# A seven-product up projection for the feed-forward part of a two-layer hybrid encoder

## The chip, the cores and the metric

The kernel runs on one core of a Trainium2 chip. The time is device microseconds of one execution. Its engines are named as in the profile: PE (TensorE), DVE (VectorE), ACT (ScalarE), POOL (GpSimd), and SP, the queue that issues most DMAs. Every engine works through its own instructions in order and waits for others at semaphores.

## What is computed

The encoder has two layers over 16 meta tokens and 1024 input tokens of width 1024, all in fp32. In each layer an input projection feeds four mixers (a short convolution, sliding-window attention, retention, RWKV), an output projection and a layer norm follow, and then the feed-forward part with another norm. The change is in the feed-forward part:

```python
def conv_glu_ffn(h, w_up, conv_w, w_down):
    z = causal_dwconv(h @ w_up, conv_w)
    u, gate = jnp.split(z, 2, axis=-1)
    return (jax.nn.silu(gate) * u) @ w_down
```

`h` is tokens x 1024, `w_up` 1024 x 5632, `w_down` 2816 x 1024, and the convolution has three taps along the tokens.

## The kernel before, in words

The tokens of a layer are four chunks: one of 272 (16 meta and 256 others) and three of 256. Layer and chunk make eight **units**, u = 0 to 7; units 0 and 4 are the first chunks. Activations lie transposed in SBUF (`hT`: 8 feature blocks of 128 partitions by tokens). Weights are read again for each unit: SP loads tiles of 128 x 1024 fp32 (0.524 MB, 4 KB a partition, one output block of 128 features by 8 input blocks) into a ring of five slots, in the order of the table `USES`. A tile is loaded once the block that used the slot before is done.

The order of blocks on PE is written out in `all_blocks`: for each unit the output projection (`out0` to `out7`), the input projection of the next unit (25 blocks), then the **up phase** (`up0` to `up43`) and the **down phase** (`dn0` to `dn7`). Each block goes to PSUM bank 0 or 1 in turn; PE waits until the block two before has been taken out (`bank_free`), which ACT does for the projections and DVE for `out` and `dn`. Semaphore `blk` counts blocks, `evA` and `evV` what ACT and DVE have taken out.

In the up phase, a block is 8 matmuls of 128x128 weights by all tokens of the unit. ACT saves the last two columns for the next chunk's convolution and copies the block into one of four rows of `raw`. DVE applies the three taps in three instructions and multiplies with the gate, ACT computes the silu. Side programs run beside it: the RWKV, retention and attention work of the next unit is cut into steps by `yield`, and `together` issues one step of each after each step of the main program, on every engine in the same order.

POOL does little: for each unit it builds three masked operands of the RWKV part (`rwkv` on POOL), after a wait for DVE (`w_mask1`) and with `w_pool` as its result, and near the end it stores the output by DMA. PE's side step waits for `w_pool`. At the start PE runs 22 warm-up matmuls of a 128x128 constant (`WARM`, L1507).

```python
for f in range(NUP):
    rest(dense(u, f"up{f}", h))
    yield
```

## Time and profile before

| | |
|---|---|
| median of 3 runs | 3187.67 us (3187.49 to 3188.24) |
| profiled execution, span | 3186.1 us |
| PE, DVE, ACT busy | 3159.8, 1340.6, 878.3 us |
| POOL busy | 34.1 us |
| moved by DMA | 442.15 MB, mean 139 GB/s |

The runs are timed without a profile and the span is that of one profiled execution; of that execution no other time is given. "Busy" counts overlapping instructions of an engine once. A matmul's duration holds its way through the array, so two that follow each other overlap: what one costs is read from starts, or from a piece of the chain by its count.

### The profile page before, as it was taken

The page shows a single profiled execution, that of the slowest core. Times are in us where ns is not written, and L with a number is a line of the kernel's source. Part 1 is how long each engine was busy: PE and PEld are TensorE (multiplying, and loading weights), DVE is VectorE, ACT ScalarE, POOL GpSimd, SP SyncE. Part 2 cuts the span into 40 slices and gives each one's busy share as a digit, 9 for nine tenths or more (in the row PEclk, how much of TensorE's full clock was granted, in tenths as well). Part 3 has the DMA queues.
Part 4 walks back from the last instruction along what each step waited for, and adds up shares of the span by engine and source line. Part 5 has one row for each costly group of instructions (what it writes and reads, how often), then busy time and mean ns, then how long its engine had stood idle before and what let it go on. Part 6 is the DMA issues. An engine that isn't in the chain of part 4 may idle for free.

```text
span 3186.1 us, 51716 instructions
## 1 busy us (share of the span) xinstructions
PE 3159.8 (99%) x21708; PEld 2695.2 (85%) x21708; DVE 1340.6 (42%) x3192; ACT 878.3 (28%) x2644; POOL 34.1 (1%) x47
## 2 busy tenths in 40 slices
PE   9999999999999999999999999999999999999998
PEld 7788788888888888888888888888888888888887
DVE  4345551545515354163541635415453254532541
ACT  3323430324303242042430423204241043411320
POOL 0000000000000000000000000000000000000000
PEclk9999999999999999999999999999999999999999
DMA  6244344443444434444344443444334443344443
GB/s 218 85 139 131 100 133 142 148 149 103 139 152 148 142 107 151 152 147 132 107 126 153 152 131 107 152 152 152 125 127 152 156 148 119 127 153 164 163 153 114
DMA packets 137574, 442.15 MB, mean 139 GB/s; under 512 B 14832, under 2 KB 34416, under 8 KB 137088
## 3 DMA queue, kind: packets, MB, share of 16 engines
q1 hardware_dynamic: 136192, 434.65, 42.4%
q0 software_dynamic: 1152, 4.19, 0.4%
q8 instruction: 173, 2.83, 0.4%
q14 instruction: 57, 0.47, 0.1%
HBM read 427.14 MB, written 4.19 MB: 135 GB/s over the span
## 4 chain that ended last, share of the span: by engine, by line
PE 97%; DVE 2%; ACT 1%; issue 0%; DMA 0%; SPq 0%; POOL 0%; DVEq 0%; ACTq 0%
PE psum L957 67%; PE psum L1471 19%; PE psum L951 2%; PE psum L973 1%; PE psum L1233 1%; PE psum L1245 1%; PE psum L1258 1%; PE psum L1184 1%; PE psum L1306 1%; PE psum L1415 1%; PE psum L1398 0%; ACT prpt L844 0%; PE psum L1353 0%; PE psum L1367 0%; PE psum L1371 0%; PE psum L1133 0%
## 5 line engine op out<-in xcount | busy, mean ns | idle before, releaser
L957 PE MATMUL psum<-hT,slots 128*128 128x256 f32 (+2 forms) x8832 | 1986.6, 383 | 2.1 <-ACT hT L593 2.1
L957 PEld LDWEIGHTS psum<-hT,slots 128*128 128x128 f32 x8832 | 1660.8, 190 | 261.3 <-issue 16.1
L1471 PE MATMUL psum<-gT,slots 128*128 128x256 f32 (+1 forms) x2816 | 615.3, 381 | 0.0
L1471 PEld LDWEIGHTS psum<-gT,slots 128*128 128x128 f32 x2816 | 534.0, 190 | 77.5
L1576 DVE SCALAR_TENSOR_TENSOR hT<-hT,psum 128x256 f32<-128x256 f32 (+2 forms) x128 | 54.1, 423 | 612.8 <-PE psum L1471 504.1
L885 ACT ACTIVATE last<-psum 128x2 f32<-128x2 f32 x352 | 60.1, 171 | 857.7 <-PE psum L957 856.9
L957 PE MATMUL psum<-mixT,slots 128*128 128x256 f32 (+2 forms) x1024 | 226.2, 381 | 0.0
L957 PEld LDWEIGHTS psum<-mixT,slots 128*128 128x128 f32 x1024 | 194.6, 190 | 28.4
L2046 DVE TENSOR_SCALAR tmpG<-raw,par 128x256 f32<-128x256 f32 (+2 forms) x176 | 62.4, 355 | 364.5 <-ACT raw L886 364.4
L604 ACT ACTIVATE scr<-hT 128x256 f32<-128x256 f32 (+2 forms) x120 | 47.8, 421 | 586.5 <-DVE hT L1594 565.5
L2046 DVE TENSOR_SCALAR gT<-raw,par 128x256 f32<-128x256 f32 (+2 forms) x176 | 62.3, 354 | 306.9 <-ACT raw L886 306.8
L886 ACT ACTIVATE raw<-psum 128x256 f32<-128x256 f32 (+2 forms) x352 | 133.9, 380 | 0.0
L2050 DVE SCALAR_TENSOR_TENSOR tmpG<-raw,par,tmpG 128x256 f32<-128x256 f32 (+2 forms) x176 | 86.5, 491 | 6.3
L2048 DVE SCALAR_TENSOR_TENSOR tmpG<-raw,par,tmpG 128x256 f32<-128x256 f32 (+2 forms) x176 | 86.4, 491 | 6.3
L2050 DVE SCALAR_TENSOR_TENSOR gT<-raw,par,gT 128x256 f32<-128x256 f32 (+2 forms) x176 | 85.8, 487 | 6.3
L2048 DVE SCALAR_TENSOR_TENSOR gT<-raw,par,gT 128x256 f32<-128x256 f32 (+2 forms) x176 | 85.7, 487 | 6.3
L580 ACT ACTIVATE rows<-psum 128x256 f32<-128x256 f32 (+1 forms) x80 | 31.0, 387 | 181.2 <-PE psum L957 181.2
L1636 DVE TENSOR_TENSOR gT<-rows 128x256 f32<-128x256 f32 (+1 forms) x56 | 24.1, 430 | 130.6 <-ACT rows L636 77.0
L878 ACT ACTIVATE tmpG<-tmpG 128x256 f32<-128x256 f32 (+2 forms) x176 | 73.8, 419 | 12.8 <-DVE tmpG L2050 12.4
L2040 DVE TENSOR_TENSOR gT<-gT,tmpG 128x256 f32<-128x256 f32 (+2 forms) x176 | 74.0, 421 | 1.2
L618 ACT ACTIVATE hT<-hT,par 128x256 f32<-128x256 f32 (+2 forms) x120 | 60.7, 589 | 39.0 <-DVE hT L1614 39.0
L580 ACT ACTIVATE gT<-psum 128x256 f32<-128x256 f32 (+1 forms) x56 | 21.5, 384 | 128.9 <-PE psum L957 128.9
(260 smaller groups left out, 2255.7 us busy)
## 6 DMA issues: line engine op xcount, KB each, us to landing
slots<-in_weights SPq DMA_DIRECT2D x792, 512.0 KB, 3.4
hT<-in_x SPq DMA_DIRECT2D x8, 512.0 KB, 5.1
out<-prpt POOLq DMA_DIRECT2D x8, 512.0 KB, 3.1
tab<-in_tables SPq DMA_DIRECT2D x6, 512.0 KB, 5.3
raw<-rows SPq DMA_DIRECT2D x24, 128.0 KB, 2.4
gT<-rows SPq DMA_DIRECT2D x24, 64.0 KB, 2.0
con<-in_consts SPq DMA_DIRECT2D x1, 1434.0 KB, 10.8
tab<-in_tables SPq DMA_DIRECT2D x2, 544.0 KB, 5.5
```

The source lines that it names most:

```text
L618: act(hT[:, m, t0:t0 + n], hT[:, m, t0:t0 + n], ACT.Identity, bias=gb[:, KD + m:KD + m + 1], scale=gb[:, m:m + 1]).then_inc(S["ln_hT"], 1)
L878: act(tmpG[:, m % 2, :n], tmpG[:, m % 2, :n], ACT.Silu).then_inc(S["g_silu"], 1)
L885: act(last2[:, u % 2, f, :], psum[:, i % 2, n - 2:n], ACT.Copy)
L886: act(buf[:, 2:2 + n], psum[:, i % 2, :n], ACT.Copy).then_inc(S["evA"], 1)
L951: return pe.transpose(dst, src, ident[:n, :n])
L957: ins = mm(psum[:, i % 2, :n], lhsT, rhs, start=k == 0, stop=k == len(pairs) - 1)
L1471: ins = mm(psum[:, i % 2, :n], w[:, e * P:(e + 1) * P], gT[:, k, first:first + n], start=k == 0, stop=k == KF - 1)
L1576: stt(x, x, ALPHA, psum[:, i % 2, :n], ALU.mult, ALU.add).then_inc(S["evV"], 1)
L2040: tt(gT[:, m, :n], gT[:, m, :n], tmpG[:, m % 2, :n], ALU.mult).then_inc(S["glu"], 1)
L2046: k = step(ts(y, src[:, 2:2 + n], par[:, w + 2:w + 3], None, ALU.mult))
L2048: k = step(stt(y, src[:, 1:1 + n], par[:, w + 1:w + 2], y, ALU.mult, ALU.add))
L2050: stt(y, src[:, 0:n], par[:, w:w + 1], y, ALU.mult, ALU.add).then_inc(S["fconv"], 1)
```

## The change

Units 1, 2, 3, 5, 6 and 7 (`seven(u)`) compute the up projection in a form of fast matrix multiplication; units 0 and 4 keep the old one. The 44 output blocks are 11 groups of 4. In a group the weights are a 2 x 2 matrix of blocks A11, A12, A21, A22 (two output blocks by four input blocks each), the activations a 2 x 2 matrix (four feature blocks by 128 tokens). Seven products of such blocks replace eight, and each is 8 matmuls of 128 columns into half a bank. The order is `STEPS7`.

Four of the products use sums of weight blocks (S1 to S4). POOL makes these in HBM (`wsum`, 11 x 4 x 0.524 MB a layer): `copy_blocks` issues 12 DMAs from HBM to HBM, `sum_blocks` 12 accumulating ones in three rounds, and POOL waits for the copies, round one and round two before what follows. Those of layer 0 stand between POOL's masks of unit 0 and unit 1, those of layer 1 between the masks of unit 1 and unit 2. SP waits for a layer's sums before its first load of one, in units 1 and 5. Four sums of activations (`tsum`) are made by DVE, late in the next unit's input projection, for unit 7 in unit 6's down phase.

Some products fall into the same PSUM range and accumulate there (`start` only for s = 0, 1, 5). ACT copies products 0, 1, 2 and 6 into `raw` (1 and 6 negated); DVE adds or subtracts products 3, 4 and 5 onto rows of `raw` straight out of PSUM, and copies the halo columns. `raw` has eight rows, and DVE convolves a group while the next is multiplied. The up phase of a changed unit has 77 weight tiles instead of 44. The DMA descriptor scratch is set smaller, which makes room in SBUF.

```diff
+def seven(u):
+
+    return u % NCH != 0
+
+
+GROUPS = NUP // 4
+FAST = [u for u in range(NU) if seven(u)]
+STEPS7 = ["A11", "S1", "S2", "S4", "S3", "A12", "A22"]
+SUMS = ["S1", "S3", "S2", "S4"]
+SUM_PARTS = [(0, 4), (4, 8), (8, GROUPS)]
+
+
+def up_names(u):
+
+    return [f"us{g}_{s}" for g in range(GROUPS) for s in range(7)] if seven(u) else [f"up{f}" for f in range(NUP)]
+
...
-    return name[:3] == "out" or name[:2] == "dn"
+    return name[:3] == "out" or name[:2] == "dn" or name[:2] == "us" and name[-1] in "345"
...
-        raw = sb("raw", 4 * (CW + 2))[:, :].rearrange("p (r t) -> p r t", r=4)
+        raw = sb("raw", 8 * (CW + 2))[:, :].rearrange("p (r t) -> p r t", r=8)
+        tsum = sb("tsum", 2048)[:, :].rearrange("p (j k t) -> p j k t", j=4, k=4)
+        wsum = nc.dram_tensor("wsum", (DEPTH, GROUPS, 4, P, 1024), F32, kind="Internal").ap()
...
+        def product_at(base, s):
+
+            return bank((base + s) % 2)[:, 0:2 * P]
...
-                sp.dma_start(slots[:, i % SLOTS, :], weights[l, which]).then_inc(s_slot[i % SLOTS], 16)
+                if name[:2] == "us":
+                    if name == "us0_1" and u == l * NCH + 1:
+                        done = 16 * len(SUM_PARTS) * (l + 1)
+                        sp.wait_ge(S["ws_first"], 2 * done)
+                        sp.wait_ge(S["ws_second"], done)
+                        sp.wait_ge(S["ws_third"], done)
+                    source = weights[l, which] if STEPS7[int(name[-1])][0] == "A" else wsum[l, which[0], which[1]]
+                else:
+                    source = weights[l, which]
+                sp.dma_start(slots[:, i % SLOTS, :], source).then_inc(s_slot[i % SLOTS], 16)
...
+            def copy_blocks(l):
+
+                for part in SUM_PARTS:
+                    for kind, first in (("S1", "A21"), ("S3", "A11"), ("S2", "A11"), ("S4", "A12")):
+                        g.dma_start(block_of(l, kind, part), block_of(l, first, part)).then_inc(S["ws_copy"], 16)
+
+            def sum_blocks(l):
+                n = len(SUM_PARTS)
+                g.wait_ge(S["ws_copy"], 16 * 4 * n * (l + 1))
+                for part in SUM_PARTS:
+                    for kind, more in (("S1", "A22"), ("S3", "A21")):
+                        g.dma_start(block_of(l, kind, part), block_of(l, more, part), accum_op=ALU.add).then_inc(S["ws_first"], 16)
+                g.wait_ge(S["ws_first"], 16 * 2 * n * (l + 1))
+                for part in SUM_PARTS:
+                    g.dma_start(block_of(l, "S2", part), block_of(l, "S1", part), accum_op=ALU.add).then_inc(S["ws_second"], 16)
+                g.wait_ge(S["ws_second"], 16 * n * (l + 1))
+                for part in SUM_PARTS:
+                    g.dma_start(block_of(l, "S4", part), block_of(l, "S2", part), accum_op=ALU.add).then_inc(S["ws_third"], 16)
+
             rwkv(0)
+            copy_blocks(0)
+            sum_blocks(0)
             for u in range(NU):
                 if u + 1 < NU:
                     rwkv(u + 1)
+                if u == 0:
+                    copy_blocks(1)
+                    sum_blocks(1)
...
+                if seven(u):
+                    for g in range(GROUPS):
+                        base, r0 = AT[u, f"us{g}_0"], 4 * (g % 2)
+                        one, two = raw[:, r0:r0 + 2, :], raw[:, r0 + 2:r0 + 4, :]
+                        a.wait_ge(S["fconv"], NUP * u + max(4 * g - 4, 0))
+                        act(raw[:, r0:r0 + 4, 0:2], last2[:, (u - 1) % 2, 4 * g:4 * g + 4, :], ACT.Copy)
+                        dst = {0: one[:, :, 2:2 + P], 1: two[:, :, 2 + P:2 + 2 * P], 2: one[:, :, 2 + P:2 + 2 * P], 6: two[:, :, 2:2 + P]}
+                        for s in range(7):
+                            src = product_at(base, s).rearrange("p (m t) -> p m t", m=2)
+                            if s in (0, 1, 2, 6):
+                                a.wait_ge(S["blk"], base + s + 1)
+                            if s in (1, 6):
+                                act(dst[s], src, ACT.Identity, scale=-1.0).then_inc(S["evA"], 1)
+                            elif s in (0, 2):
+                                act(dst[s], src, ACT.Copy).then_inc(S["evA"], 1)
+                            if g and s in (2, 4):
+                                silu(2 * g - 2 + (s == 4))
+                            if s in (1, 3, 5, 6):
+                                yield
...
+            def up_by_seven(u, h):
+
+                old, new = [x[:, 0:P] for x in h], [x[:, P:2 * P] for x in h]
+                t1, t3, t2, t4 = ([tsum[:, j, k, :] for k in range(4)] for j in range(4))
+                moving = [old[:4], t1, t2, new[4:], t3, old[4:], t4]
+                for g in range(GROUPS):
+                    base = AT[u, f"us{g}_0"]
+                    for s in range(7):
+                        w = next_slot()
+                        bank_free(base + s)
+                        if g == 0 and s == 1:
+                            pe.wait_ge(S["tsum"], 4 * (FAST.index(u) + 1))
+                        dst = product_at(base, s)
+                        for e in range(2):
+                            for k in range(4):
+                                ins = mm(dst[:, e * P:(e + 1) * P], w[:, (4 * e + k) * P:(4 * e + k + 1) * P], moving[s][k],
+                                         start=s in (0, 1, 5) and e == 0 and k == 0, stop=k == 3, skip_group_check=True)
+                        ins.then_inc(S["blk"], 1)
...
+                tt(tsum[:, 0], b11, b12, ALU.subtract).then_inc(S["tsum"], 1)
+                yield
+                tt(tsum[:, 1], b22, b12, ALU.subtract).then_inc(S["tsum"], 1)
+                yield
+                v.wait_ge(S["tsum"], before + 2)
+                stt(tsum[:, 2], tsum[:, 1], -1.0, b11, ALU.mult, ALU.subtract).then_inc(S["tsum"], 1)
+                yield
+                v.wait_ge(S["tsum"], before + 3)
+                stt(tsum[:, 3], tsum[:, 2], -1.0, b21, ALU.mult, ALU.subtract).then_inc(S["tsum"], 1)
...
+                            if g and s < 3:
+                                for f in ((4 * g - 4, 4 * g - 3), (4 * g - 2,), (4 * g - 1,))[s]:
+                                    conv(f, raw[:, 4 * ((g - 1) % 2) + f % 4, :])
+                            if s == 3:
+                                v.wait_ge(S["evA"], FREED[base + 2])
+                                v.wait_ge(S["blk"], base + 4)
+                                tt(one[:, :, 2 + P:2 + 2 * P], one[:, :, 2 + P:2 + 2 * P], part[3], ALU.add).then_inc(S["evV"], 1)
+                            if s == 4:
+                                v.wait_ge(S["blk"], base + 5)
+                                tt(two[:, :, 2 + P:2 + 2 * P], two[:, :, 2 + P:2 + 2 * P], part[4],
+                                   ALU.subtract).then_inc(S["evV"], 1)
+                                v.wait_ge(S["evV"], FREED[base + 4])
+                                v.tensor_copy(last2[:, u % 2, 4 * g:4 * g + 4, :], raw[:, r0:r0 + 4, 2 * P:2 * P + 2])
+                            if s == 5:
+                                v.wait_ge(S["blk"], base + 6)
+                                tt(one[:, :, 2:2 + P], one[:, :, 2:2 + P], part[5], ALU.add).then_inc(S["evV"], 1)
+                            if g and s in (3, 5):
+                                glu(2 * g - 2 + (s == 5))
+                            if s == 6:
+                                v.wait_ge(S["evA"], FREED[base + 6])
+                                v.wait_ge(S["evV"], FREED[base + 5])
+                            if s in (1, 3, 5, 6):
+                                yield
...
+    up = up.reshape(DEPTH, GROUPS, 2, 2, P, 2, 4, P).transpose(0, 1, 2, 5, 4, 3, 6, 7)
...
-    nc = bacc.Bacc("TRN2", target_bir_lowering=False, num_devices=1)
+    nc = bacc.Bacc("TRN2", target_bir_lowering=False, num_devices=1, dynamic_dma_scratch_size=2048)
```

The places where the order moves are these. PE, at the start of unit 1's up phase, before (L957 is the matmul of all projections, L1165 and L951 are side work):

```order
L957 MATMUL psum<-hT,slots 128x256 [waits evA,slot1_loaded]
L957 MATMUL psum<-hT,slots 128x256 x7
L957 MATMUL psum<-hT,slots 128x256 [waits evA,slot2_loaded,ln_hT]
L957 MATMUL psum<-hT,slots 128x256 x7
L1165 MATMUL psum<-con,rows 128x64 [waits w_yc,w_znew,w_yTc,n_var_out,smallA,n_mean_out,smallV]
L1165 MATMUL psum<-con,rows 128x64 x31
L951 MATMUL psum<-con,rows 128x128 [waits r_qd,evA,r_rope,smallA,in_hT,a_mix]
L951 MATMUL psum<-con,rows 128x128 x3
L957 MATMUL psum<-hT,slots 128x256 [waits evA,slot3_loaded]
L957 MATMUL psum<-hT,slots 128x256 x7
```

and now (L1577 is the new product, L1262 and L1048 the same side work):

```order
L1577 MATMUL psum<-hT,slots 128x128 [waits evA,slot2_loaded,ln_hT]
L1577 MATMUL psum<-hT,slots 128x128 x7
L1577 MATMUL psum<-tsum,slots 128x128 [waits tsum,evA,slot3_loaded]
L1577 MATMUL psum<-tsum,slots 128x128 x7
L1262 MATMUL psum<-con,rows 128x64 [waits w_yc,w_znew,w_yTc,n_var_out,smallA,n_mean_out,smallV]
L1262 MATMUL psum<-con,rows 128x64 x31
L1048 MATMUL psum<-con,rows 128x128 [waits r_qd,evA,r_rope,smallA,in_hT,a_mix]
L1048 MATMUL psum<-con,rows 128x128 x3
L1577 MATMUL psum<-tsum,slots 128x128 [waits evA,slot4_loaded]
L1577 MATMUL psum<-tsum,slots 128x128 x7
L1577 MATMUL psum<-hT,slots 128x128 [waits evA,slot0_loaded]
L1577 MATMUL psum<-hT,slots 128x128 x7
```

Each side step stands behind two products of half the columns, and the second product needs `tsum`. On POOL, from the masks of unit 0 on (`w_mask1` is DVE's mask), before:

```order
L544 TENSOR_TENSOR wset<-wset,con 128x8x64 [waits w_mask1]
L546 TENSOR_TENSOR wset<-wset,con 128x512 [waits w_unit]
L549 TENSOR_TENSOR wset<-wset,con 128x512 [waits w_t0]
L544 TENSOR_TENSOR wset<-wset,con 128x8x64 [waits w_mask1]
L546 TENSOR_TENSOR wset<-wset,con 128x512 [waits w_unit]
L549 TENSOR_TENSOR wset<-wset,con 128x512 [waits w_t0]
```

and now:

```order
L591 TENSOR_TENSOR wset<-wset,con 128x512 [waits w_t0]
L615 DMA wsum<-in_weights 128x4x1024 x8
L615 DMA wsum<-in_weights 128x3x1024 x4
L622 DMA wsum<-in_weights 128x4x1024 [waits ws_copy]
L622 DMA wsum<-in_weights 128x4x1024 x3
L622 DMA wsum<-in_weights 128x3x1024 x2
L625 DMA wsum<-wsum 128x4x1024 [waits ws_first]
L625 DMA wsum<-wsum 128x4x1024
L625 DMA wsum<-wsum 128x3x1024
L628 DMA wsum<-wsum 128x4x1024 [waits ws_second]
L628 DMA wsum<-wsum 128x4x1024
L628 DMA wsum<-wsum 128x3x1024
L586 TENSOR_TENSOR wset<-wset,con 128x8x64 [waits w_mask1]
```

The 24 DMAs of layer 0 now stand between the masks of unit 0 and unit 1, with a wait ahead of each round.

## Rows read from the trace of the kernel before

**Rows 1.** The page: span, busy shares, granted clock.
```profile
span 3186.1 us, 51716 instructions
PE 3159.8 (99%) x21708; PEld 2695.2 (85%) x21708; DVE 1340.6 (42%) x3192; ACT 878.3 (28%) x2644; POOL 34.1 (1%) x47
...
PEclk9999999999999999999999999999999999999999
```

**Rows 2.** The page: the chain that ended last, by engine and line.
```profile
PE 97%; DVE 2%; ACT 1%; issue 0%; DMA 0%; SPq 0%; POOL 0%; DVEq 0%; ACTq 0%
PE psum L957 67%; PE psum L1471 19%; PE psum L951 2%; PE psum L973 1%; PE psum L1233 1%; PE psum L1245 1%; PE psum L1258 1%; PE psum L1184 1%; PE psum L1306 1%; PE psum L1415 1%; PE psum L1398 0%; ACT prpt L844 0%; PE psum L1353 0%; PE psum L1367 0%; PE psum L1371 0%; PE psum L1133 0%
```

**Rows 3.** The chain in time, 820 to 970 us: start us, us, what.
```profile
824.12 58.71 PE psum L957 x272
```

**Rows 4.** Groups by line and form, PE and PEld: busy us, mean ns.
```profile
L957 PE MATMUL psum<-hT,slots 128*128 128x256 f32 x6624 | 1470.2, 381 | 0.0
...
L957 PE MATMUL psum<-hT,slots 128*128 128x258 f32 x704 | 158.7, 383 | 0.0
...
L957 PEld LDWEIGHTS psum<-hT,slots 128*128 128x128 f32 x8832 | 1660.8, 190 | 261.3 <-issue 16.1 <-ACT hT L593 2.4
```

**Rows 5.** Warm-up: chain in time, all its records, durations, then DMA there.
```profile
10.49 2.12 PE psum L1507 x19
...
5.76 7.29 PE psum L1507 x44
...
L1507 PEld LDWEIGHTS psum<-con x20: 192/192/192, 10.3 to 12.4; 128*128 128x128 f32 x20
...
10.20:12.60 2.40, 2.40 (x23) 2.40 (x23) 1.00 1.02 415
```

**Rows 6.** The chain in time, 690 to 720 us, two pieces of up products.
```profile
700.86 3.65 PE psum L957 x16
...
710.95 3.46 PE psum L957 x16
```

**Rows 7.** Groups by form: DVE over the span, then ACT from 695 to 878 us.
```profile
L2050 DVE SCALAR_TENSOR_TENSOR gT<-raw,par,gT 128x256 f32<-128x256 f32 x132 | 64.0, 485 | 4.7
...
L2046 DVE TENSOR_SCALAR gT<-raw,par 128x256 f32<-128x256 f32 x132 | 46.5, 353 | 227.5 <-ACT raw L886 227.4
...
L1576 DVE SCALAR_TENSOR_TENSOR hT<-hT,psum 128x256 f32<-128x256 f32 x104 | 43.7, 421 | 509.3 <-PE psum L1471 432.2 <-PE psum L957 77.0
...
L1865 DVE TENSOR_TENSOR wset<-psum,con 128x512 f32<-128x512 f32 x24 | 16.4, 683 | 8.7 <-PE psum L1194 6.8 <-PE psum L1184 1.9
...
L883 ACT ACTIVATE raw<-last 128x2 f32<-128x2 f32 x42 | 8.6, 204 | 0.0
...
L885 ACT ACTIVATE last<-psum 128x2 f32<-128x2 f32 x41 | 7.0, 171 | 87.3 <-PE psum L957 87.2
```

**Rows 8.** Busy us of the engines in three stretches, clock, DMA share, GB/s.
```profile
core 0: us, PE busy (x) PEld busy (x) DVE busy (x) ACT busy (x) POOL busy (x), PEclk, DMA share, GB/s
117.00:310.00 193.00, 191.39 (x1758) 158.40 (x1757) 96.36 (x230) 61.90 (x164) 3.23 (x3) 1.00 0.39 123
310.00:710.00 400.00, 398.80 (x2646) 332.50 (x2648) 167.18 (x391) 115.24 (x335) 3.24 (x3) 1.00 0.41 134
695.00:878.00 183.00, 181.19 (x1675) 153.44 (x1674) 94.73 (x221) 72.03 (x237) 3.24 (x3) 1.00 0.37 120
```

**Rows 9.** Timeline of POOL: start us, us, what, idle before and its end.
```profile
115.70 1.10 POOL L549 TENSOR_TENSOR wset<-wset,con 128x512 f32<-128x512 f32 x1
299.98 1.09 POOL L544 TENSOR_TENSOR wset<-wset,con 128x512 f32<-128x512 f32 x1 [183.17 <-DVE wset L1865]
```

**Rows 10.** Timeline of PE: the first side matmuls that read POOL's result.
```profile
313.05 1.15 PE L1233 MATMUL psum<-wset 64*64 64x64 f32 x32
```

**Rows 11.** DMA issues: KB each, median us from issue to landing.
```profile
slots<-in_weights SPq DMA_DIRECT2D x792, 512.0 KB, 3.4
...
out<-prpt POOLq DMA_DIRECT2D x8, 512.0 KB, 3.1
```

More of the change, by code:

```diff
@@ L138, in all_blocks @@
         out += [(u + 1, name) for name in in_order(u + 1)]
-        out += [(u, f"up{f}") for f in range(NUP)]
+        out += [(u, name) for name in up_names(u)]
         if u == NU - 2:
@@ L142, in all_blocks @@
         out += [(u, f"dn{m}") for m in range(KD)]
-    out += [(NU - 1, f"up{f}") for f in range(NUP)]
+    out += [(NU - 1, name) for name in up_names(NU - 1)]
     return out + [(NU - 1, f"dn{m}") for m in range(KD)]
@@ L190, in all_uses @@
         elif name[:2] == "up":
-            out.append((l, N_IN + KD + int(name[2:]), u, name, None))
+            f = int(name[2:])
+            if f % 2 == 0:
+                out += [(l, N_IN + KD + f + half, u, f"up{f + 1}", None) for half in range(2)]
+        elif name[:2] == "us":
+            g, s = map(int, name[2:].split("_"))
+            kind = STEPS7[s]
+            if kind[0] == "A":
+                out.append((l, N_IN + KD + 4 * g + {"A11": 0, "A12": 1, "A22": 3}[kind], u, name, None))
+            else:
+                out.append((l, (g, SUMS.index(kind)), u, name, None))
         elif name == "dn0":
@@ L519, in _ @@
                     load_input(i - 3, sp)
-                if name == "up0" and u == NU - 1:
+                if name == "us0_0" and u == NU - 1:
                     sp.wait_ge(S["blk"], AT[NU - 1, "out7"] + 1)
@@ L878, in silu @@
                     act(tmpG[:, m % 2, :n], tmpG[:, m % 2, :n], ACT.Silu).then_inc(S["g_silu"], 1)
+                if seven(u):
[17 more added lines that the diff above has]
+                                yield
+                    silu(KF - 2)
+                    silu(KF - 1)
+                    return
                 for f in range(NUP):
@@ L1454, in up @@
                 pe.wait_ge(S["ln_hT"], KD * (nth_norm(2 * u) + 1))
-                for f in range(NUP):
-                    rest(dense(u, f"up{f}", h))
-                    yield
+                if seven(u):
+                    yield from up_by_seven(u, h)
+                    return
+                for f in range(0, NUP, 2):
+                    w = [next_slot(), next_slot()]
+                    for e in range(2):
+                        rest(feature(u, f"up{f + e}", [(w[k // 4][:, 512 * e + k % 4 * P:512 * e + (k % 4 + 1) * P], h[k])
+                                                       for k in range(KD)]))
+                        yield
[11 more added lines that the diff above has]
+                        dst = product_at(base, s)
+                        for e in range(2):
+                            for k in range(4):
[4 more added lines that the diff above has]
+                            yield
             def down(u):
@@ L1618, in project @@
                 l, c0 = layer_of(u), u % NCH == 0
+                sums = token_sums(u - 1) if u and seven(u - 1) else iter(())
                 mu_at = {name: i for i, name in enumerate(["r0", "r1", "k0", "k1", "v0", "v1", "lo"])}
@@ L1741, in project @@
                         rest(short_conv(u, int(name[2])))
+                    if i >= 18:
+                        next(sums, None)
                     if name == "sq0":
@@ L2050, in up @@
                     stt(y, src[:, 0:n], par[:, w:w + 1], y, ALU.mult, ALU.add).then_inc(S["fconv"], 1)
+                if seven(u):
+                    for g in range(GROUPS):
+                        base, r0 = AT[u, f"us{g}_0"], 4 * (g % 2)
+                        one, two = raw[:, r0:r0 + 2, :], raw[:, r0 + 2:r0 + 4, :]
+                        part = [product_at(base, s).rearrange("p (m t) -> p m t", m=2) for s in range(7)]
+                        for s in range(7):
+                            if g and s < 3:
[19 more added lines that the diff above has]
+                                v.wait_ge(S["evV"], FREED[base + 5])
+                            if s in (1, 3, 5, 6):
+                                yield
+                    for f in range(NUP - 4, NUP):
+                        conv(f, raw[:, 4 * ((GROUPS - 1) % 2) + f % 4, :])
+                        if f % 2:
+                            glu(f // 2)
+                    return
@@ L2051, in up @@
+                for f in range(NUP):
+                    m, s = divmod(f, 2)
+                    v.wait_ge(S["evA"], FREED[AT[u, f"up{f}"]])
+                    conv(f, raw[:, f % 4, :])
                     if s and m:
@@ L2065, in down @@
                         ln_normalize(2 * u + 2)
+                    if u == NU - 2 and q in DOWN_ENDS and DOWN_ENDS[q] == 6:
+                        rest(token_sums(u + 1))
                     yield
```

23 lines of the change are left out of this document (20 added, 3 removed).

## The prediction

> **What bounds the kernel now.** I read the page's head first, [rows 1]: PE is busy 99% of the span, DVE 42%, ACT 28%, and the granted clock is full in all 40 slices. The chain that ended last, [rows 2], is 97% PE, 67% of it on the line that the projections share. The tables so far say that only work taken from PE, or put in its way, moves the end.
>
> What a matmul costs PE is its distance to the next, not its duration. In a stretch of the up phase of unit 1, [rows 3], 272 records of 256 columns take 58.71 us, that is 215.8 ns each, although one lasts 379 ns by [rows 4]. A logical fp32 matmul of the code is two records: the up phase of the one unit with 258 columns, 44 products of 8 matmuls, has 704 records [rows 4]. A changed unit has as many, of 256 columns. The stretch holds 17 products, each with its semaphore waits, and its mean of 215.8 ns leaves no room for a price of a wait that is already met.
>
> **The PE term.** Six of eight units change: 704 records of 256 columns become 77 products x 8 x 2 = 1232 records of 128 columns. The only 128x128 fp32 stream with a weight load per matmul is the warm-up. Late in it 19 records take 2.12 us, 111.6 ns each [rows 5]. Its operands are one constant, and the real ones differ in every matmul; the weight loads last 192 ns each there and still pass at 111.6 ns [rows 5]. Before: 704 x 215.8 = 151.9 us a unit. After: 1232 x 111.6 = 137.5 us. Gain 14.4 us, six times: **-87 us**. Bounds: half of the wide spacing (107.9) would give 6 x 19.0 = -114; at 123.3 ns nothing is left. I take the measured stream, since its shape and type are those of the new products.
>
> Where PE turns from side work to a product, the first weight load may show: pieces of 16 records last 3.46 us or 3.65 [rows 6], 0.19 more. The number of turns (44 a unit) stays, but more products lie between them. I add **+5 us**, between 0 and 6 x 33 x 0.1 = 20.
>
> **DVE and ACT.** ACT loses per unit 88 small halo copies (171 ns, and 44 of about 204) and gains 11; large evacuations stay 44 [rows 7]. DVE gains per unit 33 adds out of PSUM, priced by its PSUM-reading residual of the same 256 columns, 421 ns, and 11 tiny copies: 33 x 0.42 = 13.9 us, plus at most 11 x 0.42. DVE was busy 94.7 of 183 us in that phase and ACT 72.0 [rows 8]; with 19 more in about 169 us DVE is at 67%. The four token sums are 128x512, nearest row 0.68 us [rows 7], 2.8 us a unit, in the next unit's input projection, and in unit 6's down phase for the last; DVE is 58% idle over the span [rows 1]. Cover: PE's own stream. Taken at 0; their price if the cover fails is a rival below. The two units that keep the old product only read the same weights from two slots in another layout: 0. The scratch size changes no instruction that PE waits for: 0.
>
> **POOL, the term I trust least.** Per layer, POOL now issues copies of 4 kinds x 11 groups x 0.524 MB = 23.1 MB from HBM to HBM, then three rounds of accumulating DMAs (11.5, 5.8 and 5.8 MB), waiting for each round before the next. Behind the last wait stand POOL's three mask instructions of unit 1. Before, POOL is done with unit 0 at 116.8 us, and starts the next at 300.0 [rows 9]; PE first uses that result at 313.05 [rows 10], so POOL may come at 309.8 at the latest (3.3 us of work). That is a window of 193 us for copies, round one and round two (round three is only issued). The stream of weights holds 39% of the 16 DMA engines there [rows 8], which leaves 193 x 0.61 = 118 us of all engines.
>
> The trace has no HBM-to-HBM copy and no accumulation. The full rate is 415 GB/s with a share of 1.02 [rows 5], 158 ns for 4 KB on an engine. Copies at that rate: 23.1 / 0.415 = 56 us. An accumulation reads two inputs for each output, so I take twice: 17.3 MB x 2 / 0.415 = 83 us. Sum 139, over by 21, and three completions at 3.1 us (the landing of POOL's stores, [rows 11]) make 9: **+30 us** of PE standing still. Low bound: both at the full rate, 97 us, less than 118, so 0. High bound: copies at half rate and accumulations at a third, 111 + 125 + 9 - 118 = 127 us. Layer 1's rounds stand between the masks of unit 1 and unit 2: 400 us at 41% [rows 8], 236 us free; even the high bound (236 + 9) nearly fits.
>
> For what a rule says of the rate: the Trainium skill (DMA: Bandwidth & Descriptors, Latency and other measured facts) lists copies between HBM tensors at 207 to 214 GB/s. No row here shows it; by it the copies alone would need 108 to 111 us and the stall would be near the rival's price below.
>
> **Sharing the DMA engines.** Every weight tile is 128 rows of 4 KB, 8 an engine. If each piece of the stream waits for one accumulating piece of 316 ns, a tile takes 8 x (158 + 316) = 3.79 us against PE's 16 x 0.2158 = 3.45: +0.34. Layer 1's rounds have 352 pieces an engine, 44 tiles, **+15 us**; beside copies of 158 ns it is 2.5 us and free. Low 0; high, at 474 ns, 1.6 x 44 = 70. In the new phase a tile is wanted each 16 x 0.1116 = 1.79 us; the engines need 8 x 158 = 1.26 us, the slots hold five, and a load lands in 3.4 us [rows 11], within the four products (7.1 us) that cover it. So the stream keeps up: 0.
>
> **Sum.** Span 3186.1, and the median of the runs is 3187.7; the runs shown give no other time of the profiled execution, so the 1.6 us between the two are what lies around the span. No term changes them. 3187.7 - 87 + 5 + 30 + 15 = **3151 us**.
>
> **Rivals.**
> Sums are hidden: the DMA engines accumulate at the full rate. For it: the low bound fits the window; against: two reads for a write. 3187.7 - 87 = 3101, to 3106 with the turns.
> POOL holds the kernel up (the other side): HBM-to-HBM traffic at half rate. PE stops in unit 0's up phase, at unit 1's first side product that needs POOL's mask until round two has landed. 3187.7 - 87 + 5 + 127 + 70 = 3303 us. The gain is used up once stall and sharing together pass 82 us, that is once the work before round two exceeds 118 - 9 + 82 - 15 = 176 us of all engines. For it: [rows 9] show how soon the next mask is due; against: the window has 118 us free.
> DVE is late at the bank: with two banks in turn, the adds of products 3, 4 and 5 must end within one product, 1.79 us, after three convolution instructions of 353 and twice about 485 ns [rows 7] and side work. If each costs PE one add, 6 x 33 x 0.42 = 83, so 3234 us.
> Weight loads bound PE: at the 190 ns of their rows [rows 4], 1232 x 0.190 = 234 us a unit, +82, six times 493: 3731 us with the other terms. Against it stands the late warm-up. The Trainium skill (TensorE: Matmul & The Clock Gate, Back-to-back issue gap) gives 81 ns for pairs of load and matmul at 128 columns, against 56 for an isolated matmul; as a ratio on 111.6 ns that is an estimate of 161 ns, +280 us. The trace does not agree: its 111.6 ns already has a load in every pair.
>
> **Chances.** Forecast 0.46, hidden sums 0.14, POOL holds up 0.28, DVE late 0.07, weight loads 0.05. The measurement can tell about 0.2%, 6.4 us, from no change. POOL's case runs from my forecast's edge to its high bound, so 0.03 of it still ends faster and 0.05 within 0.2%; with the 0.46 and 0.14 that is faster 0.63, same 0.05, slower 0.32. The range goes from the hidden case with a slightly closer spacing, 3095, to the high price of POOL's case, 3300; it leaves out the weight loads, the very end of POOL's case and spacings near 108. The forecast's own range is 3115 to 3180.
>
> **What would show it.** Right: narrow records at 112 ns in products of 1.79 us from unit 1's up phase on; one idle stretch of PE near 313 us, of about 30 us, ended by POOL; tile times above 3.5 us while POOL accumulates. Wrong: spacing above 123 ns; a stall of 80 us or more (then DMA rates were the failed term); idle PE before the products after 3, 4 and 5, ended by DVE; or PE waiting for DMA inside the new up phases.

## The result and the profile after

The changed kernel takes 3197.7 us (median of 8 runs), the kernel before 3188.0 us in the same rounds; the ratio is 1.0028, 95% interval 1.0018 to 1.0037. It is slower by 0.28%, and the interval leaves out 1. One of the eight runs took 6305.69 us at a mean granted clock of 0.48 and does not enter the ratio; the other seven lie between 3195.2 and 3199.1 us. The forecast was 3151 us and faster. The profiled execution has a span of 3195.6 us and a time of 3197.37 us.

The page of the changed kernel answers to [rows 1, 2]:

```profile
span 3195.6 us, 58419 instructions
PE 3087.7 (97%) x24876; PEld 2745.9 (86%) x24876; DVE 1436.9 (45%) x3480; ACT 844.6 (26%) x2180; POOL 82.3 (3%) x95
...
PEclk9999699999999999999999999999999999999999
...
PE 86%; issue 6%; DVE 3%; DMA 2%; ACT 1%; POOL 1%; SPq 0%; DVEq 0%; ACTq 0%
```

PE's busy time fell by 72 us, and the span rose by 9.5. The chain lost 11 points of PE: "issue", DMA and POOL now stand in it, since from the stall it goes back through POOL's queue. The fifth slice of the clock row, 320 to 399 us, is at 6: PE stood there.

Who made PE wait, longest in total first (us in total, times, longest):

```profile
PE psum L1330 <- POOL wset L591: 50.7, 1, 50.7
PE psum L1577 <- ACT raw L968: 8.0, 9, 3.3
PE psum L1054 <- DMA slots<-in_weights: 6.4, 3, 3.5
PE psum L1230 <- DVE Zb L1996: 5.9, 5, 1.4
PE psum L1054 <- issue: 5.9, 4, 2.1
PE psum L1631 <- DMA con<-in_consts: 5.7, 1, 5.7
```

In the kernel before, the only wait over 3 us was the first load. Now there is one of 50.7 us for POOL's mask. POOL's timeline around it, answering to [rows 9] (start us, us, what, idle before and its end):

```profile
115.51 1.10 POOL L591 TENSOR_TENSOR wset<-wset,con 128x512 f32<-128x512 f32 x1
116.55 2.40 POOL L615 DMA_DIRECT2D wsum<-in_weights  x3
...
214.72 1.33 POOL L622 DMA_DIRECT2D wsum<-in_weights  x1 [16.12 <-DMA wsum<-in_weights]
...
311.99 1.27 POOL L625 DMA_DIRECT2D wsum<-wsum  x1 [12.87 <-DMA wsum<-in_weights]
...
349.83 1.26 POOL L628 DMA_DIRECT2D wsum<-wsum  x1 [18.77 <-DMA wsum<-wsum]
363.93 2.54 POOL L628 DMA_DIRECT2D wsum<-wsum  x2 [12.84 <-issue]
365.45 2.14 POOL L586 TENSOR_TENSOR wset<-wset,con 128x512 f32<-128x512 f32 x1
```

The copies are issued from 116.6 us; round one starts at 214.7 when they have landed, round two at 312.0, round three at 349.8. Between the first and the other two DMAs of round three POOL stands 12.8 us for "issue", that is for nothing that it waits for in its program. It stood so among the copies too: the fourth, the seventh and the eleventh were issued at 140.8, 167.2 and 197.1 us, and up to these times POOL's queue had moved 6.29, 12.58 and 19.92 MB, just what the three, six and ten copies ahead of each hold. Its mask comes at 365.5 in place of 300.0 us, and PE's first side matmul that needs it, at 313.05 us before [rows 10], runs at 369.95 us.

The stretches of the trace, from the first matmul of each phase to the first of the next, show where the time went (us; the middle column is the run without POOL's DMAs, told below):

| stretch | before | without POOL's DMAs | changed |
|---|---|---|---|
| first input projections, to the first output projection | 176.5 | 176.5 | 178.7 |
| input projection of unit 1 with up phase of unit 0 | 265.6 | 265.6 | 331.3 |
| input projection and up phase, unit 1 | 284.4 | 276.9 | 282.2 |
| the same, units 2 and 3 | 281.0, 299.0 | 269.4, 286.3 | 269.4, 286.3 |
| the same, units 5 and 6 | 284.4 each | 272.9 each | 272.9 each |
| up phase of unit 7 | 154.6 | 142.7 | 144.3 |

Units 2, 3, 5 and 6 gain 11.5 to 12.7 us each. The loss is in the first 770 us, and most of it in one phase.

The new form itself, in a stretch that no side work enters, answers to [rows 3]:

```profile
2427.15 51.81 PE psum L1577 x464
```

464 records in 51.81 us are 111.7 ns each, with different weights and tokens in every one, as in the warm-up.

### The profile page after: what moved, and what is told of

Same layout as the page of the kernel before. It is cut to its first block, busy times and chain, and to the rows that moved or that the text cites. A ratio compares the mean times of both kernels' runs of the same rounds, so it can differ in the third digit from the quotient of the medians.

```text
span 3195.6 us, 58419 instructions
## 1 busy us (share of the span) xinstructions
PE 3087.7 (97%) x24876; PEld 2745.9 (86%) x24876; DVE 1436.9 (45%) x3480; ACT 844.6 (26%) x2180; POOL 82.3 (3%) x95
## 3 DMA queue, kind: packets, MB, share of 16 engines
q1 hardware_dynamic: 164704, 538.48, 50.7%
q0 software_dynamic: 24448, 96.47, 11.9%
## 4 chain that ended last, share of the span: by engine, by line
PE 86%; issue 6%; DVE 3%; DMA 2%; ACT 1%; POOL 1%; SPq 0%; DVEq 0%; ACTq 0%
PE psum L1054 33%; PE psum L1577 24%; PE psum L1595 19%; PE psum L1048 1%; PE psum L1070 1%; DMA wsum<-in_weights 1%; PE psum L1330 1%; PE psum L1342 1%; PE psum L1355 1%; DMA wsum<-wsum 1%; DMA slots<-in_weights 1%; PE psum L1403 0%; PE psum L1512 0%; PE psum L1281 0%; PE psum L1495 0%
## 5 line engine op out<-in xcount | busy, mean ns | idle before, releaser
L1054 PE MATMUL psum<-hT,slots 128*128 128x256 f32 (+2 forms) x4608 | 1050.9, 387 | 12.8 <-issue 5.9
L1054 PEld LDWEIGHTS psum<-hT,slots 128*128 128x128 f32 x4608 | 871.6, 191 | 160.8 <-issue 16.2
L1577 PE MATMUL psum<-tsum,slots 128*128 128x128 f32 x4224 | 520.2, 278 | 11.1 <-ACT raw L968 8.0
L1577 PEld LDWEIGHTS psum<-tsum,slots 128*128 128x128 f32 x4224 | 493.6, 193 | 23.3 <-issue 20.9
L1577 PE MATMUL psum<-hT,slots 128*128 128x128 f32 x3168 | 388.3, 276 | 0.9 <-DVE raw L2211 0.9
L1577 PEld LDWEIGHTS psum<-hT,slots 128*128 128x128 f32 x3168 | 370.1, 192 | 3.1 <-issue 1.6
L966 ACT ACTIVATE raw<-psum 128x256 f32<-128x256 f32 x132 | 50.6, 383 | 294.7 <-PE psum L1577 294.7
L968 ACT ACTIVATE raw<-psum 128x256 f32<-128x256 f32 x132 | 50.3, 381 | 174.9 <-PE psum L1577 174.4
L982 ACT ACTIVATE last<-psum 128x2 f32<-128x2 f32 x88 | 15.0, 171 | 270.0 <-PE psum L1054 269.8
```

Of the source, the lines that this page charges most:

```text
L966: act(dst[s], src, ACT.Identity, scale=-1.0).then_inc(S["evA"], 1)
L968: act(dst[s], src, ACT.Copy).then_inc(S["evA"], 1)
L1054: ins = mm(psum[:, i % 2, :n], lhsT, rhs, start=k == 0, stop=k == len(pairs) - 1)
L1577: ins = mm(dst[:, e * P:(e + 1) * P], w[:, (4 * e + k) * P:(4 * e + k + 1) * P], moving[s][k], start=s in (0, 1, 5) and e == 0 and k == 0, ...
```

## The experiments

Two theories stood at first. A: PE stands because POOL's masks of unit 1 are queued behind the sums. B: the traffic of the sums slows what runs beside it, wherever it is put.

### The masks ahead of the rounds

```diff
             rwkv(0)
             copy_blocks(0)
+            rwkv(1)
             sum_blocks(0)
...
-                if u == 0:
+                if u == 1:
                     copy_blocks(1)
+                if u == 2:
                     sum_blocks(1)
```

> Edit: POOL makes the masks of unit 1 after the copies of layer 0 and ahead of its three accumulating rounds, and layer 1's copies and rounds come after the masks of units 2 and 3. Theory A (PE stands because POOL's masks of unit 1 stand behind the rounds): the 50.7 us wait of PE for POOL goes, and with it the slow restart, so 3197.7 - 51 - 5 = about 3142 us, and the stretch of the second input projection and first up phase, 331 us in the changed kernel and 266 before, comes down to about 280. Rival B (the rounds slow everything beside them by their traffic, so the wait only moves): the rounds now run beside PE at full demand and cost as much there; 3180 us or more, with waits for weight loads of 30 us or more.

Measured: 3173.9 us, ratio 0.9957 (0.9942 to 0.9972). PE does not wait for POOL at all, and the second input projection with the first up phase takes 271.7 us in place of 331.3, better than I expected. But it is 32 us over the expected time, and the loss has a new place: unit 2's new up phase takes 225.2 us instead of 178.2. PE's waits in that phase, 1077 to 1303 us:

```profile
PE psum L1579 <- DMA slots<-in_weights: 17.9, 10, 3.1
PE psum L1579 <- DMA slots<-wsum: 14.1, 9, 2.1
```

and three stretches (busy us and count of PE, PEld, DVE, ACT, POOL, then PE's clock, DMA share, GB/s): beside the copies of layer 1, and beside its rounds.

```profile
700.00:880.00 180.00, 174.32 (x2238) 166.92 (x2238) 107.00 (x260) 65.08 (x164) 12.10 (x15) 0.99 0.94 348
1090.00:1180.00 90.00, 87.58 (x1377) 80.91 (x1375) 51.98 (x126) 34.92 (x84) 8.84 (x8) 1.00 1.01 276
1180.00:1300.00 120.00, 88.07 (x673) 83.90 (x674) 46.79 (x117) 18.66 (x52) 8.83 (x7) 0.90 1.04 296
```

Beside the copies, unit 1's up phase takes 184.5 us, 1.2 less than without any of POOL's DMAs: nothing is lost. Beside the rounds the DMA engines are full (1.04) and PE is busy 88 of 120 us. Of the 47 us, 32.0 are waits for loads; a mean granted clock of 0.90 over 120 us can hold up to 12 more, an estimate. Layer 0's rounds cost 6.1 us beside the old up phase (271.7 against 265.6). A was right on the wait; B was right that rounds have a price of their own, and it is 47 us where PE wants a tile each 1.8 us.

### Without POOL's DMAs

```diff
             rwkv(0)
-            copy_blocks(0)
-            sum_blocks(0)
...
-    source = weights[l, which] if ... else wsum[l, which[0], which[1]]
+    source = weights[l, which if ... else N_IN + KD + 4 * which[0] + which[1]]
```

> Leaves out all of POOL's copies and sums; the products that use sums read other weight tiles of the same size from the inputs, so the output is not the reference's. Theory A: what is left is the price of the seven-product form alone. Units 2, 3, 5, 6 took 11.5 to 12.7 us less than before each and unit 7 10.3; six units give about -70, so 3188 - 70 = 3118 us. Rival B (the form itself loses at its evacuations and loads, and the gain seen in late units is an accident of the order): 3150 us or more. Rival C (my term of 14.4 us a unit was right and the traffic took the rest, in late units too): 3101 to 3106 us.

Measured: 3122.3 us, ratio 0.9794 (0.9778 to 0.9810). That is 65.6 us under the kernel before, near A (70); B and C are out. The form gains 10.9 us a unit, not 14.4 less 0.8. What is left of PE's waits there:

```profile
PE psum L1569 <- ACT raw L960: 8.0, 9, 3.3
PE psum L1222 <- DVE Zb L1988: 5.9, 5, 1.4
...
PE psum L1569 <- DVE raw L2206: 3.1, 2, 2.3
```

8.0 + 3.1 us for evacuations by ACT and DVE, and 5.9 us for an RWKV step on DVE, which cost 1.7 us before: about 15 us more waiting than before, and 16 us are missing from the 82 of the forecast. That the two are the same is read from the sizes; no run takes these waits away.

### Rounds that only copy

```diff
-    g.dma_start(block_of(l, kind, part), block_of(l, more, part), accum_op=ALU.add)
+    g.dma_start(block_of(l, kind, part), block_of(l, more, part))
```

> The three rounds move the same bytes between the same places as plain copies; nothing is added, so the output is not the reference's. Theory A (an accumulation reads twice and costs an engine about twice a copy): rounds one and two of layer 0, 135 us in the changed kernel, take about 70, and PE's wait for POOL falls from 51 us to under 5; about 3145 us. Rival B (accumulating costs what copying costs, and the time is that of any traffic between two places in HBM): the rounds take as long as now and the time is within 5 us of 3197.

Measured: 3129.7 us (one run), and no wait of PE for POOL. Rounds one and two of layer 0 last from 218.0 to 296.7 us, 79 us against 135. POOL's queue in the changed kernel and in this one (packets, MB, share of 16 engines):

```profile
q0 software_dynamic: 24448, 96.47, 11.9%
```

```profile
q0 software_dynamic: 24448, 96.47, 8.5%
```

The same packets and bytes hold the engines 11.9% of 3195.6 us in one and 8.5% of 3127.9 in the other, 249 and 174 ns a packet. With half of the packets accumulating, such a one costs about 174 + 2 x 75 = 324 ns, an estimate. The first two rounds alone show it directly: from 214.7 to 349.8 us 4368 packets of POOL's queue held 66.8% of the 16 engines, 331 ns each, and the plain ones 58.1% from 218.0 to 296.7 us, 167 ns each. Theory A holds: twice a copy, as the forecast took it (316). The time is 15 us under the expected one, because here the rounds are cheap for the stream too: with plain rounds all of POOL's traffic costs 7.5 us by the spans (3127.9 against 3120.4). Adding is what makes them dear.

### Room for descriptors

```diff
-    nc = bacc.Bacc("TRN2", ..., dynamic_dma_scratch_size=2048)
+    nc = bacc.Bacc("TRN2", ..., dynamic_dma_scratch_size=4096)
```

> Only the scratch for descriptors is doubled to 4096. In the changed kernel POOL is held inside the issue of a round: it issues one DMA, stands 12.8 us, and issues the last two of round three, although nothing ahead of it is waited for. Theory A (room for descriptors holds it): with twice the room round three is issued without a stand, the masks of unit 1 come about 13 to 15 us earlier, PE's wait falls from 51 to about 37 us, and the time is about 3183 us. Rival B (POOL stands until data has moved, whatever the room): no change, 3195 to 3199 us.

Measured: 3163.2 us (one run), 20 us lower than expected, and 34.6 under the changed kernel. POOL's rounds here:

```profile
209.20 3.88 POOL L622 DMA_DIRECT2D wsum<-in_weights  x3 [31.85 <-DMA wsum<-in_weights]
257.45 3.74 POOL L622 DMA_DIRECT2D wsum<-in_weights  x3 [44.38 <-issue]
297.49 3.81 POOL L625 DMA_DIRECT2D wsum<-wsum  x3 [36.30 <-DMA wsum<-in_weights]
335.13 3.82 POOL L628 DMA_DIRECT2D wsum<-wsum  x3 [33.83 <-DMA wsum<-wsum]
337.43 2.65 POOL L586 TENSOR_TENSOR wset<-wset,con 128x512 f32<-128x512 f32 x1
```

Three DMAs of a round are issued at once and round three without a stand. What comes ahead is faster too: the copies take 93 us, not 98, rounds one and two 126, not 135, and the masks come at 337.4 instead of 365.5 us. PE's wait is 22.1 us, and unit 1's input projection and up phase take 275.7 us instead of 282.2. Theory B is out and A was too narrow: the small room cost the stand, and speed as well.

To part the two I kept the small scratch and moved round three alone, for both layers:

```diff
                 g.wait_ge(S["ws_second"], 16 * n * (l + 1))
+
+            def last_round(l):
                 for part in SUM_PARTS:
...
                     rwkv(u + 1)
                 if u == 0:
+                    last_round(0)
                     copy_blocks(1)
                     sum_blocks(1)
+                if u == 1:
+                    last_round(1)
```

> Edit to the changed kernel alone: round three is issued after the masks of unit 1 (and, for layer 1, of unit 2) instead of ahead of them; scratch as it was, 2048. POOL stood 12.8 us inside the issue of round three. Theory A (the small scratch costs twice: a stand in the issue of round three, and slower rounds one and two, since few DMAs can be under way): PE's wait falls by about 15 us, from 51 to 36, and the time to about 3181 us; the other 14 us of the 29 that the doubled scratch took off the wait belong to the rounds. Rival B (all of it was the stand in round three): PE's wait falls by about 29 us to 22, as with the doubled scratch, about 3168 us.

Measured: 3176.6 us, ratio 0.9962 (0.9947 to 0.9976). PE waits 33.8 us for POOL:

```profile
PE psum L1335 <- POOL wset L591: 33.8, 1, 33.8
```

A holds; the time fell by 21 us for 17 of waiting. POOL began the masks at 347.6 us instead of 365.5: 15.6 of these 18 us are the issue of round three with its stand (349.8 to 365.5), and 2 come from rounds that were done earlier. With the larger scratch the issue of round three takes 2.3 us, so 13 of the 28 us by which its masks came earlier are the stand, and the other 15 the faster copies and rounds.

### Where the rounds should run

```diff
             copy_blocks(0)
+            rwkv(1)
             sum_blocks(0)
...
-                if u == 0:
+                if u == 3:
                     copy_blocks(1)
                     sum_blocks(1)
...
-    nc = bacc.Bacc("TRN2", ..., dynamic_dma_scratch_size=2048)
+    nc = bacc.Bacc("TRN2", ..., dynamic_dma_scratch_size=4096)
```

This kernel is the "e5" of the expectations further down, and the base of the four edits that follow; all of them have the scratch of 4096.

> Edit: the masks of unit 1 go between the copies and the rounds of layer 0; layer 1's copies and rounds come after the masks of unit 4, so that its rounds fall into the down phase of unit 3 and the input projection of unit 4, where PE takes a weight tile each 3.5 us; the scratch is 4096. The first call showed 3122.3 us without POOL's DMAs and 47 us lost in unit 2's new up phase when layer 1's rounds ran beside it. Theory A (what rounds cost depends on the phase they run beside: dear beside the new up phase with a tile each 1.8 us, cheap beside the others): 3122 + 2 for the copies + 6 for layer 0's rounds + 6 for layer 1's = about 3136 us, no wait of PE for POOL. Rival B (the rounds cost 25 us or more a layer wherever they run): 3165 us or more.

Measured: 3152.2 us, ratio 0.9884 (0.9870 to 0.9899). 16 us over A and 13 under B, so neither holds as it stood. Layer 0's rounds cost 4.4 us beside the old up phase, a little less than the 6 expected. Layer 1's copies and rounds cost 8.1 us in unit 3's up phase, into which the end of the copies and the start of round one still fell, 6.2 us in unit 3's down phase (82.2 against 76.0), and 11.5 us in the input projection of unit 4 with the up phase behind it. One wait for a weight load holds 8.3 us:

```profile
PE psum L1055 <- DMA slots<-in_weights: 8.3, 1, 8.3
```

Both layers early, against e5:

```diff
             rwkv(1)
             sum_blocks(0)
+            copy_blocks(1)
+            sum_blocks(1)
             for u in range(NU):
...
-                if u == 3:
-                    copy_blocks(1)
-                    sum_blocks(1)
```

> Edit: POOL makes the masks of unit 1 after the copies of layer 0, and then everything else ahead of the masks of unit 2: layer 0's rounds, layer 1's copies and rounds; scratch 4096. By the earlier runs the rounds of layer 0 end near 445 us, the copies of layer 1 near 540 and its rounds near 665, before the new up phase of unit 1 starts near 694 and before PE wants the masks of unit 2 near 715. Theory A (what a round costs depends on the phase beside it: 4 to 11 us beside phases with a weight tile each 3.5 us, 47 beside the new up phase, and an order that keeps all of it off the new up phases is the cheapest): 3122 + 1 (copies) + 5 + 6 = about 3134 us, PE's wait for POOL zero. Rival B (in the up phase of unit 0 the rounds of both layers add up, as the 16 us lost there beside the doubled scratch suggest): 3145 us or more.

Measured: 3165.1 us, ratio 0.9928 (0.9915 to 0.9942). Theory A missed by 31 us, and B's 3145 or more holds. The copies began at 429.6 us, but layer 1's rounds began at 569 us, where 540 was reckoned, and the third was only issued at 694.6, where 665 was reckoned for the end: unit 1's input projection took 112.3 us instead of 91.2, with two waits for loads of 15.1 us together, and its new up phase 198.3 instead of 185.7, with 8.8 us of waits for the tiles of sums. The sums of layer 0 had long been there, so the loss is one of traffic.

One unit later than in e5:

```diff
-                if u == 3:
+                if u == 4:
                     copy_blocks(1)
```

> The kernel of e5 with layer 1's copies and rounds one unit later, after the masks of unit 5 (near 1881 us), so that they run beside the old up phase and the down phase of unit 4, and are done near 2100 us, ahead of the new up phase of unit 5 near 2250. In e5 they cost 8 us beside the new up phase of unit 3 and 11.5 us in the input projection of unit 4, of which 8.3 us are one wait for a weight load; in the kernel with both layers early the same place, an input projection, cost 21 us. Theory A (rounds are cheap beside an old up phase and a down phase, 4 to 6 us a layer as layer 0's were, and dear beside an input projection or a new up phase): 3122 + 1 + 5 + 5 = 3133 us. Rival B (a layer's copies and rounds cost 15 to 20 us wherever they run): 3150 us.

Measured: 3144.8 us, ratio 0.9863 (0.9846 to 0.9879). It is the best of all that give the right output, and beats both kernels, the one before by 1.4%. Yet B (3150) is nearer than A (3133), and on layer 1 too: input projection and up phase of unit 4 take 296.2 us instead of 283.9, and the down phase 79.2 instead of 76.0, 15.5 us in all. A layer's sums cost 7 us the first time and 15 the second, both beside old phases with a tile each 3.5 to 3.7 us. From 1880 to 2260 us PE waits 10.2 us in nine places on the projections' line for nothing that the profile shows. Why the second layer costs twice the first is not settled.

### The evacuations

```diff
                                 v.wait_ge(S["blk"], base + 4)
+                                extra(3, part[3])       # v.tensor_copy(more, src)
...
```

> The kernel of e5 with one more PSUM-reading copy of 256 columns (about 0.42 us) on DVE ahead of each of its 33 evacuating adds a unit, 198 in all; it changes no result. Theory A (DVE has room at the bank, what the product form loses is elsewhere): within 8 us of e5. Rival B (DVE's adds set when banks come free, so that each further one moves PE): 198 x 0.42 = 83 us, up to that much over e5.

Measured: 3156.4 us, 4.2 more than its base of 3152.2. The copies are there:

```profile
L2195 DVE COPY more<-psum 128x256 f32<-128x256 f32 x198 | 83.9, 424 | 194.2 <-PE psum L1580 193.2 <-ACT raw L971 0.8
```

83.9 us of work on DVE moved the end by 4. DVE has room at the bank; A holds.

```diff
-                            if s in (1, 3, 5, 6):
+                            if s in (2, 3, 5, 6):
                                 yield
```

> The kernel of e5 with ACT's first side step of each group moved from behind product 1 to behind product 2, so that a table load and exponentials of the attention step (3.2 us together) no longer stand ahead of the evacuation of product 2. Without POOL's DMAs PE still waits 8.0 us for ACT's copies out of PSUM and 5.9 us for a DVE step of the RWKV part. Theory A (order on ACT makes the evacuation late): the 8.0 us go, 3 to 8 us less than e5. Rival B (PE then waits for the side step itself, which is now late by one product of 1.8 us): the waits move, and the time is the same or longer than e5.

Measured: 3164.9 us, 12.7 more than its base. The wait for ACT's copies fell from 7.3 to 3.4 us, and others grew:

```profile
PE psum L1578 <- DVE raw L2212: 7.5, 4, 2.9
PE psum L1578 <- DMA slots<-in_weights: 5.9, 6, 3.1
...
PE psum L1578 <- ACT raw L969: 3.4, 4, 0.9
PE psum L1513 <- ACT prpt L927: 3.3, 5, 0.8
```

Rival B holds: the waits moved, to DVE's add behind ACT's copy, to side work of ACT and to loads. In the units without any of POOL's traffic the new up phase went from 178.2 to 180.7 us (unit 2) and from 179.9 to 182.3 (units 5 and 6). In unit 3, beside layer 1's copies, it went from 195.8 to 205.9, and unit 4 got 7 us back. The cause of ACT's lateness can be read in the changed kernel: in unit 5 a table load at 2380.6 us and four exponentials keep ACT until 2383.8, and its copy out of PSUM at 2383.92 us is what PE waited for. That this costs the whole 8 us was not shown by taking it away.

## Why the forecast was wrong

The direction was wrong; the range, 3095 to 3300, held the time, and 0.32 of the chances lay on slower. 3151 came from five terms; these are their sizes.

| term | forecast | measured | by |
|---|---|---|---|
| narrow records, six units | -87 | -66 for the whole form | run without POOL's DMAs |
| turns to side work | +5 | within the -66 | |
| PE stands for POOL | +30 | +50.7 | wait of PE for POOL |
| sharing the DMA engines | +15 | +25 | the rest of 75.5 between 3122.3 and 3197.7 |
| evacuations by ACT and DVE | 0 | about 11 of the missing 16 | waits of PE |

**The step that failed is the one on POOL, the largest miss of the sum.** Its mechanism was right, down to the place, and its prices were a little low: copies held the 16 engines for 64 us (65.2% of 98; 56 taken) and rounds one and two for 90 (66.8% of 135; 83 taken), 331 ns a piece where 316 was taken. So the forecast had round two done 30 us after POOL was due at 309.8, and it was done at 349.8, 40 us after. What failed outright is "round three is only issued", taken at nothing, and with it "the scratch size changes no instruction that PE waits for: 0". With the scratch of 2048, POOL issued its next copy only when all those before had landed, and in round three it stood 12.8 us in the same way; the issue of that round took 15.6 us, and the mask began at 365.5. PE came to its wait at 319.2 us, not at 313.05, and so waited 50.7 us. Round three moved behind the mask gives 21 us back, and the scratch doubled 34.6; either of them makes the kernel faster than the one before. By the sum the 16 us missing from the PE term would have been enough for that as well; that was not tried.

**Sharing** was priced for layer 1's rounds alone. All traffic took 2.2 us in the first input projections, 15 beside the stall in the phase with unit 0's up blocks (331.3 - 265.6 - 50.7), 5.3 in unit 1's and 1.6 in unit 7's. Where it was 15, the DMA share was 0.96 and PE restarted at a lower clock:

```profile
117.00:312.00 195.00, 187.88 (x1710) 154.85 (x1709) 94.89 (x226) 61.45 (x162) 16.16 (x19) 1.00 0.96 296
312.00:366.00 54.00, 7.22 (x61) 5.47 (x59) 4.60 (x10) 1.81 (x8) 7.13 (x7) 0.61 0.82 166
366.00:484.00 118.00, 112.85 (x1218) 90.32 (x1219) 58.53 (x132) 52.67 (x150) 13.50 (x17) 0.96 0.96 319
```

Granted 0.61 on average in the stretch in which PE stood, 0.96 in the next. The restart by itself, from 369.95 us on:

```profile
370.00:374.00 4.00, 4.00 (x49) 3.54 (x50) 0.94 (x2) 0.00 (x0) 0.00 (x0) 0.50 1.07 213
374.00:378.00 4.00, 4.00 (x16) 3.09 (x15) 0.89 (x4) 0.00 (x0) 0.00 (x0) 0.86 1.07 212
378.00:382.00 4.00, 4.00 (x87) 3.22 (x86) 1.72 (x4) 2.29 (x7) 0.00 (x0) 1.00 1.05 214
```

PE worked at the lower of the two levels, granted 0.50, for about 5 us, which costs at most 2.6, an estimate. Some 4 us were lost before the stall (from the first block of the phase PE took 93.7 us to its wait, where it had taken 89.6 to the same point). The rest lies beside layer 1's rounds, and answers to the price of sharing:

```profile
486.10 11.00 PE psum L1054 x48
497.10 1.55 issue
498.65 14.90 PE psum L1054 x64
513.56 1.09 issue
```

From 486.10 to 549.38 us, 240 records, 15 tiles, take 4.22 us a tile, where the kernel before took 3.67 (272 records in 62.34 us): 0.55 more, and 0.34 was forecast. So the mechanism and about the size were right for those tiles, 8 us in all. What the term left out is layer 0's traffic; it had the rounds of layer 1 beside 44 tiles of the stream, while a good part of them ran beside the down phase of unit 0 and the output projection, which took 80.7 and 28.5 us as before.

**The PE term** was right in its rate (111.7 ns against 111.6) and wrong in what I took at 0. DVE's adds are all but hidden: PE waits 4.0 us for them, and more of them moved the end by 4. ACT, which I had relieved of 77 small copies a unit, is late all the same at nine places, and an RWKV step on DVE (Zb) now keeps PE waiting 5.9 us in five places where it was 1.7; that the shorter steps of the main program are the reason is argued, not shown.

Of the rivals, the stopped POOL was the nearest, at 31% of the way from the forecast to its own high price; its reason, traffic within HBM at half rate, is out. "DVE late" and "weight loads" are out. The tests of the text came in, but for the length of the stall: records at 112 ns, one idle stretch, at 319 to 370 us and of 51 us instead of 30, ended by POOL, tile times above 3.67 us while POOL accumulates, no wait for loads in the new up phases as long as no round runs beside them. One reading was off and nothing rests on it: [rows 4] have a mean of 381 ns, not 379.

## What to carry to other kernels

Work that is free on the critical engine is not free in the queue that issues it: list what stands behind it there, when that is due, and how many DMAs the queue can have under way before an issue itself waits. Price a background transfer by the phase beside it, and try it there: a layer's rounds cost 4 to 6 us (layer 0) or, with its copies, 15 us (layer 1) beside old phases with a tile each 3.5 to 3.7 us, and 47 us beside a tile each 1.8 us. And when a stream is made faster, look at the side programs that were cut to its steps: they have less time for each, which is argued here and not shown.

## What was not expected of the hardware

An accumulating DMA between two places in HBM held an engine about 324 to 331 ns for 4 KB, a plain one 174 ns in the run with plain rounds, not far from the 158 ns of the loads at full rate: copies within HBM ran nearly as fast as loads into SBUF. The Trainium skill (DMA: Bandwidth & Descriptors, Latency and other measured facts) lists 207 and 214 GB/s for copies between HBM tensors issued from the sync and scalar queues, for two row pitches, and less for others. Here layer 0's 23.1 MB, issued from POOL, took from 116.6 to 214.7 us, 235 GB/s, out of 343 GB/s that the DMA engines moved in all from 117 to 215 us. So the trace is above both figures with its own layout, and they could not be taken over as a rate for it.

Doubling the scratch for descriptors from 2048 to 4096, with no other change, shortened the copies from 98 to 93 us and two rounds of accumulation from 135 to 126, and removed the stand of 12.8 us (one run). With 2048 POOL issued three or four copies and then stood until all had landed; with 4096 it issued seven, and the next at 173.7 us, when its queue had moved 14.68 MB, just those seven.
